# Token sums of a two-layer encoder trunk as 100 equal columns, in and between the output products, with adaLN parts in the pauses

## The reference

```
mod = silu(c) @ w_ada + b_ada                   # 6 x 1024: sh1, sc1, g1, sh2, sc2, g2
h = rms_norm(x, g_pre_mix) * (1 + sc1) + sh1
...                                             # mLSTM, gMLP, windowed attention -> merged
x = x + g1 * rms_norm(merged @ w_out, g_post_mix)
h2 = rms_norm(x, g_pre_ffn) * (1 + sc2) + sh2
gate, up = jnp.split(h2 @ p['w_ffn_in'], 2, axis=-1)
f = (jax.nn.silu(gate) * up) @ p['w_ffn_out']
x = x + g2 * rms_norm(f, g_post_ffn)
```

## Time and profile before

| | us |
|---|---|
| median of three runs | 2187.01 (2186.15 to 2191.91) |
| the profiled execution | 2186.8 |
| its span | 2185.0 |
| PE busy | 2139.7 (98%) |
| POOL busy | 1232.1 (56%) |
| DVE, ACT busy | 692.7, 407.2 |

### The profile page before, as it was taken

One profiled execution on the slowest core, in us unless ns is written; L12 is line 12 of the kernel. 1 busy time (PEld: TensorE's weight loads), 2 busy tenths in 40 slices (PEclk: granted clock), 3 DMA queues, 4 the chain that ended last, 5 costly groups with the idle time before them and its releaser, 6 DMA issues.

```text
span 2185.0 us, 38222 instructions
## 1 busy us (share of the span) xinstructions
PE 2139.7 (98%) x16911; PEld 2061.9 (94%) x16911; DVE 692.7 (32%) x1211; ACT 407.2 (19%) x902; POOL 1232.1 (56%) x604
## 2 busy tenths in 40 slices
PE   6999999999999999999999999999999999999998
PEld 5999898999999999999999989889999999999997
DVE  3132466522345110011453345662315521001113
ACT  2121224110132110001221121331103211111111
POOL 3244444567762666667744534446686357667663
PEclk7999999999999999999989999999999899999999
DMA  9655231223253442442221252212235123222222
GB/s 306 213 174 64 53 88 49 71 78 97 87 163 106 143 130 79 157 122 72 87 76 39 74 63 68 69 49 80 78 104 157 50 59 87 68 86 79 87 68 84
DMA packets 319829, 211.06 MB, mean 97 GB/s; under 512 B 12544, under 2 KB 292656, under 8 KB 319536
## 3 DMA queue, kind: packets, MB, share of 16 engines
q1 hardware_dynamic: 313072, 205.13, 33.5%
q10 hardware_dynamic: 6592, 3.48, 0.6%
HBM read 203.80 MB, written 4.07 MB: 95 GB/s over the span
## 4 chain that ended last, share of the span: by engine, by line
PE 94%; POOL 2%; DMA 1%; DVE 1%; ACT 1%; issue 0%; SPq 0%; DVEq 0%; ACTq 0%; POOLq 0%
PE ps L789 62%; PE ps L814 11%; PE ps L834 4%; PE ps L840 2%; PE ps L928 2%; POOL lo L743 1%; PE ps L874 1%; PE ps L856 1%; POOL hi L740 1%; DMA raw<-in_w_in 1%; PE ps L1082 1%; PE ps L1254 1%; PE ps L1213 1%; PE ps L1097 1%; PE ps L1230 1%; PE ps L1284 1%
## 5 line engine op out<-in xcount | busy, mean ns | idle before, releaser
L740 POOL TENSOR_TENSOR hi<-raw,consts 128x1024 fp32r<-128x1024 f32 (+2 forms) x260 | 467.2, 1797 | 855.9 <-PE ps L789 539.0
L743 POOL TENSOR_TENSOR lo<-raw,hi 128x1024 fp32r<-128x1024 f32 (+2 forms) x260 | 602.6, 2318 | 20.4
L789 PE MATMUL ps<-h_hi,hi 128*128 128x288 f32 x2752 | 596.3, 298 | 0.6 <-POOL lo L743 0.6
L789 PE MATMUL ps<-h_hi,lo 128*128 128x288 f32 x2752 | 589.2, 296 | 0.0
L789 PE MATMUL ps<-h_lo,hi 128*128 128x288 f32 x2752 | 588.9, 296 | 0.0
L789 PEld LDWEIGHTS ps<-h_hi,hi 128*128 128x128 f32 x2752 | 442.2, 189 | 8.0 <-issue 5.3
L789 PEld LDWEIGHTS ps<-h_hi,lo 128*128 128x128 f32 x2752 | 443.3, 189 | 0.0
L789 PEld LDWEIGHTS ps<-h_lo,hi 128*128 128x128 f32 x2752 | 443.2, 189 | 0.0
L1794 DVE TENSOR_TENSOR tmp<-sq,ps 128x576 f32<-128x576 f32 x44 | 33.2, 754 | 587.1 <-PE ps L789 579.0
L814 PE MATMUL ps<-y_hi,hi 128*128 128x288 f32 x616 | 134.5, 300 | 5.4 <-POOL lo L743 5.3
L814 PE MATMUL ps<-y_hi,lo 128*128 128x288 f32 x616 | 131.8, 296 | 0.0
(11 more groups left out here) (334 smaller groups left out, 2849.2 us busy)
## 6 DMA issues: line engine op xcount, KB each, us to landing
raw<-in_w_in SPq DMA_DIRECT2D x108, 512.0 KB
ada<-in_w_ada SPq DMA_DIRECT2D x24, 2048.0 KB, 8.9
raw<-in_w_ffn_in SPq DMA_DIRECT2D x88, 512.0 KB
raw<-in_w_ffn_out SPq DMA_DIRECT2D x32, 384.0 KB
raw<-in_w_ffn_out SPq DMA_DIRECT2D x32, 320.0 KB
raw<-in_w_out SPq DMA_DIRECT2D x16, 512.0 KB
raw<-in_w_br_mlstm SPq DMA_DIRECT2D x8, 512.0 KB
raw<-in_w_br_swa SPq DMA_DIRECT2D x8, 512.0 KB
```

The costliest lines, as they stand in the source:

```text
L740: pool.tensor_tensor(hi, RAW[s][:, 0:size], ONES[:, 0:1].to_broadcast([128, size]), ALU.mult).then_inc(chunk_hi, 1)
L743: pool.tensor_tensor(lo, RAW[s][:, 0:size], hi.bitcast(f32), ALU.subtract).then_inc(chunk_split, 1)
L789: m = pe.matmul(o[:, h, :], a[:, k, c0:c0 + 128], mv(k, h), start=(k == 0 and begins), stop=(k == nk - 1 and a is wl))
```

## The change

- A sum has 100 equal columns of ones as moving operand instead of one (`SUMW`); the readers take every hundredth column.
- The three sums from `ACC` are inside the last tile of the product, ahead of blocks 3, 6 and 7 of `wo7`, and of blocks 6, 9 and 10 of `fo1_7` of layer 0; the one that layer 1's end has is ahead of block 8 of `fo1_7`.
- An adaLN part is cut in two around the first sum of the pause: 6 blocks ahead of it, 2 behind. In pause p2 of layer 0 these are new: layer 1's part 8, and behind the second spread part 9. The stops that had them in `fi1` go; the one after `fi1_7` keeps a transpose back. Their transposes back stand after `qk4` of layer 1. Their weights go to other buffers (the region of h), loaded by SP together, ahead of the loads of `fo1_3`.
- In `out_group` the waits for the next chunk's split and the next unit stand four matmuls later, at the low weights of the last block.
- DVE takes the first row of `p1b` / `p2b` from PSUM itself.

```diff
+SUMW = 100
...
-ADA_IN.update({(1, a): 0 if a < 10 else 1 for a in range(HALVES)})
+ADA_IN.update({(1, a): 0 if a < 9 else 1 for a in range(HALVES)})
+BACK_IN = {**ADA_IN, (1, 8): 1}
...
+IN_P2 = (1, (8, 9))
...
-             "fi0_21": (1, (6,), (5,)), "fi1_3": (1, (7,), (6,)), "fi1_7": (1, (8,), (7,)), "fi1_11": (1, (9,), (8,)),
-             "fi1_15": (1, (), (9,))},
-         1: {"fi0_5": (1, (), (10, 11))}}
+             "fi0_21": (1, (6,), (5,)), "fi1_3": (1, (7,), (6,)), "fi1_7": (1, (), (7,))},
+         1: {"qk4": (1, (), (8, 9)), "fi0_5": (1, (), (10, 11))}}
...
-    return ["n1b"]
+    return ["n1b", mod(*IN_P2[:1], IN_P2[1][1])]
...
-    out = ["p1s", "p1t", "p1b", mod(lm, a), "n2b", mod(lm, b)]
+    out = ["p1s", mod(lm, a), "p1t", "p1b", "n2b", mod(lm, b)]
...
-    return out + (["p2s", "p2t", "p2b"] if l == 0 else ["p2s", "gk7"])
+    return out + (["p2s", mod(IN_P2[0], IN_P2[1][0]), "p2t", "p2b"] if l == 0 else ["p2s", "gk7"])
...
+            if lm and a in IN_P2[1]:
+                return 2 + IN_P2[1].index(a)
...
+                        if (l, c, i) == (0, 1, 3):
+                            sp.wait_ge(done_by("fi1_21"), done(0, "fi1_21"))
+                            for a in IN_P2[1]:
+                                ada_load(1, a)
...
-                        pool.wait_ge(group_done, done(0, mod(1, 9)))
+                        pool.wait_ge(group_done, done(0, mod(1, 7)))
...
-                            between[1]()
+                        if between is not None and k in between:
+                            between[k]()
...
+                            if between is not None and k in between:
+                                between[k]()
                             for a, mv, begins in ((wh, mh, True), (wh, ml, False), (wl, mh, False)):
+                                if k == k1 - 1 and a is wl:
+                                    if pos + part < NCH - 1:
+                                        pe.wait_ge(chunk_split, split_count(l, pos + part + 1))
+                                    if part:
+                                        pe.wait_ge(unit_of(*follower(name)), empty(*follower(name)))
                                 for h in range(2):
                                     m = pe.matmul(o[:, h, :], a[:, k - k0, :], mv(k, h),
...
-                        m = pe.matmul(unit(l, name)[:, c + t:c + t + 1], sq[:, t0:t0 + 128], ONES[:, 0:1],
+                        m = pe.matmul(unit(l, name)[:, c + t * SUMW:c + (t + 1) * SUMW], sq[:, t0:t0 + 128], ONES[:, 0:SUMW],
...
-                def sums(p):
+                def gathered(p):
+
+                    tile = "fo1_6" if p == "p2" else "wo6"
+
+                    def squares():
+                        pe.wait_ge(unit_of(l, p + "s"), empty(l, p + "s"))
+                        if (l, p + "t") in G:
+                            pe.wait_ge(acc1_added, nth(acc1_added, l, 6 * (p == "p2") + 5))
+                        else:
+                            pe.wait_ge(unit_of(l, p + "q6"), read(l, p + "q6"))
+                        token_sums(p + "s", 0, ACC[:, 0, :], True, False)
+
+                    def new_squares():
+                        pe.wait_ge(unit_of(l, p + "t"), empty(l, p + "t"))
+                        pe.wait_ge(unit_of(l, tile), read(l, tile))
+                        token_sums(p + "t", 512, ACC[:, 2, :], True, False)
+
+                    def products():
+                        pe.wait_ge(unit_of(l, p + "q6"), read(l, p + "q6"))
+                        token_sums(p + "t", 0, ACC[:, 1, :], True, False)
+
+                    return squares, new_squares, products
+
+                def sums(p, fill=None):
 
                     j, tile = 8 * (p == "p2"), "fo1_7" if p == "p2" else "wo7"
-                    pe.wait_ge(unit_of(l, p + "s"), empty(l, p + "s"))
-                    pe.wait_ge(unit_of(l, p + "q6"), read(l, p + "q6"))
-                    token_sums(p + "s", 0, ACC[:, 0, :], True, False)
+                    if fill is not None:
+                        modulate(*fill, range(0, 6))
                     pe.wait_ge(osq_ready, nth(osq_ready, l, j + 7))
                     token_sums(p + "s", 0, SQ[:, 0, :], False, True).then_inc(done_by(p + "s"), 1)
+                    if fill is not None:
+                        modulate(*fill, range(6, 8))
                     if (l, p + "t") in G:
-                        pe.wait_ge(unit_of(l, p + "t"), empty(l, p + "t"))
-                        token_sums(p + "t", 0, ACC[:, 1, :], True, False)
-                        token_sums(p + "t", 8, ACC[:, 2, :], False, False)
                         pe.wait_ge(gsq_ready, nth(gsq_ready, l, j + 7))
-                        token_sums(p + "t", 8, SQ[:, 1, :], False, True)
+                        token_sums(p + "t", 512, SQ[:, 1, :], False, True)
                         pe.wait_ge(unit_of(l, tile), read(l, tile))
                         token_sums(p + "t", 0, TS[:, 1, :], False, True).then_inc(done_by(p + "t"), 1)
...
+                def modulate(lm, a, ks=range(8)):
 
                     nm, s = mod(lm, a), ada_slot(lm, a)
-                    pe.wait_ge(ada_loaded[s], ada_loads(lm, a))
-                    pe.wait_ge(unit_of(l, nm), empty(l, nm))
...
+                        pe.wait_ge(unit_of(l, nm), empty(l, nm))
                     wv = ADA_BUF[s].rearrange("p (k c) -> p k c", k=8)
...
                 n = STREAM[l]
...
+                    x = gathered("p1")
+                    feature_group(f"wo{i}", P_WO + i, 8, 128, 0, *HM, lead=True,
+                                  between={3: x[0], 6: x[1], 7: x[2]} if i == 7 else None)
                 lm, fill = IN_P1[l]
-                sums("p1")
-                modulate(lm, fill[0])
+                sums("p1", (lm, fill[0]))
                 pe.wait_ge(rstd2_ready, nth(rstd2_ready, l, 1))
...
-                        out_group(f"fo{c}_{i}", pos + 2 * i, nb, *gm, moving=(gl_ready, j0) if i == 0 else None)
+                        x = gathered("p2")
+                        out_group(f"fo{c}_{i}", pos + 2 * i, nb, *gm, moving=(gl_ready, j0) if i == 0 else None,
+                                  between=({6: x[0], 9: x[1], 10: x[2]} if l == 0 else {8: x[0]}) if (c, i) == (1, 7) else None)
...
                     j0 += nb
-                sums("p2")
...
+                        nm = mod(IN_P2[0], IN_P2[1][1])
+                        dve.wait_ge(done_by(nm), done(1, nm))
                     dve.wait_ge(hh_ready, nth(hh_ready, lh, 16 * w + k))
...
 
-                    dve.wait_ge(unit_of(l, p + "b"), read(l, p + "b"))
-                    tt(OMID[:, k, :], OMID[:, k, :], R1, ALU.mult).then_inc(dve_step, step())
-
-                def added(k):
-
-                    dve.wait_ge(dve_step, step.all())
+                    if k == 0:
...
+                    if (l, i) == (1, 4):
+                        modulation_done(1, 4, (2, 64, 1.0))
```

More of the change, by code:

```diff
@@ L918, in out_tokens @@
                     token_tiles(f"gk{k}", OMID[:, k, :])
-                def modulate(lm, a):
+                def modulate(lm, a, ks=range(8)):
                     nm, s = mod(lm, a), ada_slot(lm, a)
-                    pe.wait_ge(ada_loaded[s], ada_loads(lm, a))
-                    pe.wait_ge(unit_of(l, nm), empty(l, nm))
+                    if ks[0] == 0:
+                        pe.wait_ge(ada_loaded[s], ada_loads(lm, a))
+                        pe.wait_ge(unit_of(l, nm), empty(l, nm))
                     wv = ADA_BUF[s].rearrange("p (k c) -> p k c", k=8)
-                    for k in range(8):
+                    for k in ks:
                         for x in range(4):
@@ L993, in _ @@
                     spread("n1b", 1)
+                    modulate(IN_P2[0], IN_P2[1][1])
                 n = STREAM[l]
@@ L1371, in _ @@
                     j0 += nb
-                sums("p2")
+                sums("p2", (IN_P2[0], IN_P2[1][0]) if l == 0 else None)
                 if l == DEPTH - 1:
@@ L1466, in h_hi @@
                             copy_r2(l, "n2b" if first else "n1b")
-                            if first:
-                                modulation_tile(IN_P1[l][0], IN_P1[l][1][1])
+                            lm, (_, b) = IN_P1[l] if first else IN_P2
+                            modulation_tile(lm, b)
                 def modulation_tile(lm, a):
@@ L1720, in _ @@
                 roots("p1")
+                modulation_tile(lm, fill[0])
                 roots2(l, 1)
                 copy_r1("p1")
-                modulation_tile(lm, fill[0])
                 h_hi(8, 3)
@@ L1926, in new_sums @@
                     dve.wait_ge(done_by(nm), done(l, nm))
-                    tt(UC[:, 2, :], unit(l, nm)[:, 8:13], RC[:, 0, :], ALU.mult).then_inc(dve_step, step())
+                    tt(UC[:, 2, :], sums_of(unit(l, nm)[:, 512:1012]), RC[:, 0, :], ALU.mult).then_inc(dve_step, step())
                     dve.wait_ge(dve_step, step.all())
```

(17 more changed lines are left out.)

30 lines of the change are left out of this document (13 added, 17 removed).

## The result

The changed kernel takes 2167.18 us (median; 2166.48 to 2171.16), the kernel before 2188.88 beside it: ratio 0.9903 [0.9885, 0.992], in brackets the 95% interval. In two more series it gave 0.9917 [0.9898, 0.9936] and 0.9914 [0.9899, 0.9929]. The profiled execution took 2171.16 us with a span of 2169.4: 15.6 us less than the earlier trace rows's 2185.0.

The account below looks back on a forecast made before the run. TensorE, busy 98% of the span, was taken as the bound: its work, clock and few waits. Terms -2.0 - 5.1 - 5.4 - 4.1 - 4.0 + 1.2 + 0.7 = -18.7 us from 2186.8 gave 2168 us, range 2162 to 2178.

Parts of the forecast that it names:

- p1 of layer 0: Pause p1 of layer 0, first sum to stream: 14.8 us against 16.8, so -2.0 us.
- p1 of layer 1: Pause p1 of layer 1: the same work, 14.8 us against 19.9, so -5.1 us.
- Stream behind p2: Stream behind pause p2 of layer 0, at half clock at first: 29.57 us against 26.29 behind p1, so -3.3 us.
- adaLN stops: Stops after `fi1_7`, `fi1_11` and `fi1_15`: they lose 1.96, 2.30 and 0.34 us, so -4.6 us.
- Later waits: Output product `fo0` of layer 0: eight tiles wait less for POOL's split, -4.0 us; `fo1` and layer 1 nothing.
- SP's loads: Two 2 MB loads ahead of those of `fo1_3`: hidden with little to spare, 0 taken, 0 to 5 us kept.
- DVE and ACT edits: DVE's first product from PSUM and ACT's order: nothing gained or lost, -0.2 to +0.5 us a pause.
- p2 of layer 0: Pause p2 of layer 0: 15.15 us against 17.25, so -2.1 us, with two adaLN parts now inside.
- Rival 1: Columns do not hold the clock, it falls in all pauses as before: 2183.5 us; chance 0.08.
- Rival 3: Sums inside `wo7` and `fo1_7` take the clock already there: 17.7 us a pause, 2221 us; chance 0.04.
- Rival 2: The two adaLN loads hold up `fo1_3` by 2 to 6 us: 2170 to 2174 us; chance 0.09.
- rival 4: Waits moved in `out_group` gain nothing since POOL paces the chunks: 2172 us; its shades within the forecast's 0.70.

Follow-up runs that it names:

- Columns alone: The kernel before with 100 columns per sum instead of one, order, parts and waits untouched: 2173.55 us, ratio 0.9938.
- One column: The changed kernel with one column per sum instead of 100: 2179.38 us, ratio to the kernel before 0.9961.
- waits alone: The kernel before with only the two waits in `out_group` moved to the block's last matmul: 2182.6 us, ratio 0.9971.
- the change again: The changed kernel measured again with no edit: 2169.29 us, ratio to the kernel before 0.9917.
- third: Third profile of the unedited changed kernel, run as control for later versions: 2169.87 us, ratio to the kernel before 0.9914.
- early waits: The changed kernel with the two waits in `out_group` back at the block's first matmul: 2176.13 us, ratio to the kernel before 0.9949.
- ACT's row: The changed kernel with DVE's first product from `acc` again, not from PSUM: 2171.51 us, ratio to the kernel before 0.9921.
- part's rest later: The changed kernel with the last two adaLN blocks behind the first spread and the end's sum outside the product: 2167.1 us, ratio to before 0.991.
- no parts in p2: The changed kernel with parts 8 and 9 back at their stops after `fi1_7` and `fi1_11`: 2174.08 us, ratio to the kernel before 0.9937.
- the last version: The changed kernel with all sums in the pause and the last two adaLN blocks behind the first spread: 2166.38 us, ratio to before 0.9897.
- the last three versions: The changed kernel with all sums in the pause (2164.29, again 2165.63 us), with two adaLN blocks behind the first spread (2167.1), with both (2166.38).

## Why the prediction was right, and where it was not

The time came as forecast, and its largest part, the clock in the p1 pauses and the stream, by the mechanism named; several other steps missed, in both directions. Step by step, from positions in the two traces (forecast; measured, us):

- p1 of layer 0 -2.0; -2.2. p1 of layer 1 -5.1; -5.5. Columns alone gave 13.63 - 16.81 = -3.2 and (1720.03 - 1706.40) - (1729.98 - 1709.90) = -6.4, these from its own trace and that of before: the order laid out for these pauses takes 0.9 us back in each. The forecast counted TensorE's idle 0.5 us there, but did not set it against the old order at full clock.
- Stream behind p2 -3.3; -3.4. With p1 this is the clock. One column and Columns alone show it for p1; behind p2 the columns alone did not hold it, and with the adaLN parts in p2 it held.
- adaLN stops -4.6; -5.0. Transposes back +0.5; +0.5.
- Later waits, layer 0 -4.0; 71.77 - 75.84 = -4.1. **Layer 1 nothing; -2.0.** The step that failed is "in layer 1 transposes stand between the tiles: nothing there": the earlier trace rows were read for layer 0 alone, and the rows 1877.39 and 1950.68 above were there to be read. The waits alone gave 6.3 us in time.
- End +1.2; +1.1. Splices +0.7; nothing: a sum takes 1.11 us inside the product and 3.41 / 3 = 1.14 outside.
- SP's loads 0; 0 for TensorE, though POOL's wait of 8.85 us shows that the margin was used.
- DVE and ACT edits "nothing gained or lost"; -0.4 a pause (11.57 against 11.16). It was in the forecast of 11.2 unseen, since I took the distance from spread to `hs` from a pause at half clock.
- **p2 of layer 0 -2.1; +1.0.** The step that failed is "everything is 0.35 later than in p1, so 11.55". It gave DVE's chain 1.52 us, as in p1, and did not ask what POOL does meanwhile: the chain moved 4 us nearer to the tile (10.4 to 6.5) while POOL's splits stayed where they were.
- **Elsewhere 0; +3.9**: 2.0 by 407 us, 1.9 in layer 1's mixer. Of this 1.5 each is the half clock behind the tiny matmuls that are in both kernels; the remaining 0.9 is not clock, and the change again, at full clock there, was 1.3 behind at 407 us too. The first stretch came in two of three profiles of the change, the second in all three.

Together these make 2.0 - 2.2 - 4.1 - 5.0 + 1.0 - 3.4 + 0.5 + 1.9 - 5.5 - 2.0 + 1.1 = -15.7 us, the difference of the spans (15.6) but for rounding. Forecast were -18.7. The median went down by 21.7 with an interval of 17.5 to 25; the kernel before was profiled at 2186.8 against a median of 2188.88, the change at 2171.16 against 2167.18, which is the 6 us between the two accounts. That 2168.0 met 2167.18 so closely is in part luck: the profiled pair gives 3.1 us less than forecast, the median 3 us more, and within the account misses of 2 to 4 us stand against each other.

Rival 1 fell: the clock was held in the p1 pauses in all three profiles of the change. Rival 3 fell with it: in no profile did the clock fall inside `wo7` or `fo1_7`. Rival 2's queue existed but stayed hidden, and rival 4 was the wrong way round.

**DVE's stall.** In every profile in which the step is long in p2 it ends with POOL's split, to 0.02 us: change 1116.72 and 1116.71; again 1116.04 and 1116.02; third 1116.16 and 1116.14; one column 1118.94 and 1118.93; early waits 1119.66 and 1119.64; ACT's row 1117.57 and 1117.55; part's rest later 1115.14 and 1115.12; no parts in p2 1119.18 and 1119.16; columns alone 1121.98 and 1121.97. It takes 0.81 to 2.30 us, by when in the split it begins. In the five profiles where POOL had finished, that of before among them, it takes 0.16 or 0.17. The two DVE steps ahead of it read PSUM and are not held up; this is the first whose operands both lie in SBUF. The Trainium skill, "SBUF — State Buffer", section "Who interferes with whom", says that a DVE instruction with two SBUF inputs contends with a GpSimd instruction that reads SBUF, and that one of them then waits for the whole of the other. The trace agrees, with these numbers, and over the whole program too: in the profile before, 79 TENSOR_TENSOR instructions of DVE without a PSUM operand began inside a POOL split, and none ended before it; of 138 with a PSUM operand, 84 did (after: none of 80, 97 of 138; in all 14 profiles together 7 of 1115 without a PSUM operand did). A row of the kernel before, which I had passed over, shows it plainly:
```profile
1275.31 2.40 POOL L743 TENSOR_TENSOR lo<-raw,hi 128x1024 fp32r<-128x1024 f32 x1
1275.36 2.44 DVE L1794 TENSOR_TENSOR den<-den,em_cols 128x4 f32<-128x4 f32 x2
```
That moving the sums takes the stall away is shown; a version that keeps the sums in the product and holds POOL's split back instead was not tried, nor one that leaves the adaLN part whole between the spreads, as columns alone has it in p1, where the held step cost nothing.

Open is why the stretch in layer 1's mixer loses its clock. The one at 151 us goes by the execution: it came in five of the 14 profiles, columns alone and the last version among them, 490 us ahead of the first instruction that any edit touches. The one in the mixer is less clear. It came in all three profiles of the change, with one column, with early waits and with ACT's row, and not in the kernel before, with late waits alone, columns alone, no parts in p2, or in the four profiles of the last three versions.

## What to carry to other kernels

TensorE that is busy by the profile can still lose its clock: look at the granted clock beside the busy time, and give reductions over partitions a wide operand where they stand together, here 100 columns at 0.15 us a sum over one. Put a wait in front of the instruction that needs it, not of the block, and count every place where it stands, in every layer. Test the parts of a change alone: here the new order cost time that the columns had won. Work that covers a wait for other engines is worth most where that wait is. When a pause is shortened, the small DVE steps in it move into what GpSimd is doing there: look for its long SBUF instructions, whose rest each DVE step with two SBUF operands can have to wait out, and for the clock behind that wait.

## What the runs showed of the hardware that was not expected

- One-column fp32 sums, TensorE busy 2.00 of 2.00 us, took the clock to 0.50; sums of 100 columns in the same place left it at 1.00. The Trainium skill, "TensorE: Matmul & The Clock Gate", section "Part 1: The HAM clock gate", has it fall after idling; here TensorE was never idle, and the measurement decides. Behind a wait of 1.64 us it fell during sums of 100 columns too (No adaLN parts in p2, 1114.4).
- Some 2 us of 4x4 transposes and one-column matmuls between full products (1204.6 to 1206.6) were followed by 3.4 us at half clock in some versions and not in others, with the same instructions.
- A sum of 100 columns costs 1.11 to 1.19 us against 1.04 for one column, at full clock.
- A DVE step of 128x5 took up to 2.30 us, the rest of a GpSimd split of 128x1024, where both its operands were in SBUF, and 0.16 otherwise.
